# A fused two-block layer on one core: how the in-projection's matmuls are dealt out among the steps of a recurrence

## The reference

```
h  = x * (1 + scale) + shift                 # scale, shift, gate = silu(c) @ mod_w[l] + mod_b[l]
a, r0, k0, v0, wd, ad, gate = split(h @ ev_w_in)
for d in (forward, backward):
    r, k, v = token_shift(r0), token_shift(k0), token_shift(v0)
    decay, a = lora(wd), lora(ad)
    S = S * decay + (S @ a) b^T + v k^T      # one 64 x 64 state for each of 16 heads
    y = S @ r;  y = group_norm(y) + bonus
out = concat(pool(a), y_fwd + y_bwd) * silu(gate) @ ev_w_out
```

## Time and profile before

| what | value |
|---|---|
| median of three runs | 3863.41 us |
| the profiled execution, its own time | 3858.04 us |
| its span, first to last instruction | 3856.2 us |
| granted TensorE clock, mean over the span | 0.965 |
| PE busy (matmuls) | 3547.2 us, 92% |
| PEld busy (weight loads) | 2932.6 us, 76% |
| DVE busy | 2038.4 us, 53% |
| ACT busy | 1541.8 us, 40% |
| POOL busy | 250.7 us, 6% |
| the two-lane recurrence with its fill | about 190 to 1440 us of the span |

### The profile page before, as it was taken

How to read it: one execution, slowest core, us unless ns; L and a number is a source line. 1 busy time by engine, 2 the same in 40 slices (tenths; PEclk the granted TensorE clock), 3 DMA queues, 4 the chain that set the end, 5 groups by cost and what they waited for, 6 DMA issues and landing times. The chain is left out here.

```text
span 3856.2 us, 71009 instructions
## 1 busy us (share of the span) xinstructions
PE 3547.2 (92%) x31292; PEld 2932.6 (76%) x31292; DVE 2038.4 (53%) x3564; ACT 1541.8 (40%) x2599; POOL 250.7 (6%) x295
## 2 busy tenths in 40 slices
PE   6788989999898998989999799989999999999998
PEld 3566666766666676768888789847989799999877
DVE  1454454544455447774665556655444555555444
ACT  2333343333333333454544444425443444444433
POOL 0001111011111112002000000010000000000000
PEclk9899999999999999999999799999999999999999
DMA  9423323242333416443325354414553555555554
GB/s 379 144 70 97 112 86 117 70 128 84 117 101 97 128 44 234 151 138 113 109 91 185 128 164 136 154 61 155 184 181 125 175 175 175 182 180 185 190 182 163
DMA packets 349473, 548.57 MB, mean 142 GB/s; under 512 B 11724, under 2 KB 119916, under 8 KB 346988
## 3 DMA queue, kind: packets, MB, share of 16 engines
q1 hardware_dynamic: 346716, 538.78, 42.9%
q10 hardware_dynamic: 2448, 5.24, 0.4%
HBM read 535.86 MB, written 8.13 MB: 141 GB/s over the span
## 5 line engine op out<-in xcount | busy, mean ns | idle before, releaser
L302 PE MATMUL lane<-r,r 128*128 128x256 f32 (+1 forms) x8520 | 1506.9, 326 | 50.4 <-DVE r L260 40.4
L260 DVE TENSOR_TENSOR r<-ring,r 128x1024 fp32r<-128x1024 f32 x770 | 941.2, 1229 | 944.9 <-ACT r L299 943.6
L302 PEld LDWEIGHTS lane<-r,r 128*128 128x128 f32 x8520 | 1279.5, 193 | 207.7 <-DVE r L260 45.7
L302 PE MATMUL bank<-r,r 128*128 128x512 f32 (+2 forms) x6360 | 1402.2, 359 | 36.3 <-DVE r L260 24.8
L302 PEld LDWEIGHTS bank<-r,r 128*128 128x128 f32 x6360 | 1055.0, 195 | 241.9 <-issue 52.2
L299 ACT ACTIVATE r<-ring 128x1024 fp32r<-128x1024 f32 x770 | 808.8, 1056 | 957.1 <-PE lane L302 570.9
L302 PE MATMUL lane<-arena 64*64 64x64 f32 (+4 forms) x12940 | 622.6, 254 | 68.3 <-DVE arena L260 23.9
L302 PEld LDWEIGHTS lane<-arena 64*64 64x64 f32 (+3 forms) x12940 | 468.7, 140 | 234.2 <-issue 111.1
L299 ACT ACTIVATE arena<-lane 128x256 f32<-128x256 f32 (+3 forms) x578 | 248.8, 451 | 558.5 <-PE lane L302 446.4
L260 DVE TENSOR_TENSOR arena<-arena 128x256 f32<-128x256 f32 (+7 forms) x568 | 255.6, 481 | 35.8 <-ACT arena L299 14.9
L271 DVE COPY arena<-lane 128x256 f32<-128x256 f32 (+3 forms) x366 | 131.8, 362 | 267.2 <-PE lane L302 249.6
(11 more groups left out here) (94 smaller groups left out, 1252.2 us busy)
## 6 DMA issues: line engine op xcount, KB each, us to landing
ring<-in_w_gate_up SPq DMA_DIRECT2D x88, 1024.0 KB, 5.0
ring<-in_mod_w SPq DMA_DIRECT2D x73, 1024.0 KB, 5.2
ring<-in_ev_w_in SPq DMA_DIRECT2D x44, 1024.0 KB, 8.4
ring<-in_w_down SPq DMA_DIRECT2D x44, 1024.0 KB, 5.0
ring<-in_od_w_in SPq DMA_DIRECT2D x40, 1024.0 KB, 5.1
ring<-in_w_in SPq DMA_DIRECT2D x40, 1024.0 KB, 5.1
ring<-in_w_xkv SPq DMA_DIRECT2D x32, 1024.0 KB, 5.3
ring<-in_ev_w_out SPq DMA_DIRECT2D x28, 1024.0 KB, 5.2
```

What stands on the lines that cost most here:

```text
L260: return Nothing() if self.e is None else self.e.tensor_tensor(o, a, b, op)
L302: return Nothing() if self.e is None else self.e.matmul(o, l, r, start=start, stop=stop)
```

## The change

The FILL table is larger, the split of a fill between the sources is no longer a share but follows the blocks, and the loads and splits stand elsewhere in the list. The diff, cut to its core:

```
-FILL = {"shift": 4, "kk_sum": 6, "keys": 4.5, "turn_AV": 2, "P_LR": 1, "KR0": 1, "KR1": 1, "solve": 0.5, "GH": 1,
-        "QY": 1, "state0": 2, "state1": 2, "state2": 2, "state3": 2, "centre": 3, "gn_sum": 6, "read_out": 2}
-MOD_SHARE = 0.125
+FILL = {"shift": 5.5, "kk_sum": 7.5, "keys": 6, "turn_AV": 3, "P_LR": 1.5, "KR0": 1, "KR1": 1.5, "double0": 0.5, "solve": 0.5,
+        "GH": 1, "QY": 1, "state0": 2, "state1": 2, "state2": 2, "state3": 2, "centre": 3, "gn_sum": 6.5, "read_out": 3.5}
...
+    def load_mod():
+        if mod_todo and not mod_pieces:
+            l, g, k0 = mod_todo.pop(0)
+            mod_pieces.append((l, g, k0, piece("mod_w", l, k0, 4, g * 512, 512, ring_mod)))
+
     def modulations():
+        while mod_todo or mod_pieces:
+            load_mod()
+            l, g, k0, pc = mod_pieces.pop(0)
             if k0 == 0:
                 b = bank(mod_turn)
             step("mod", l, g, pc, k0, b)
             if k0 == KT - 4:
                 step("mod_row", l, g, b)
-                yield False
+            yield
+            if k0 == KT - 4:
                 step("mod_col", l, g, bank(mod_turn))
...
-                if sm.kind == "gate_in":
-                    step("load_lora", hp)
...
+        def split_next():
+            if not halves:
+                more()
+            if halves:
+                hp, sm, pc, h = halves.pop(0)
+                split_.append((hp, blocks(pc, 1024 * h, h == 1, [(sm, 8 * h + k) for k in range(8)])))
+                if not halves:
+                    more()
+
         while True:
-            while len(split_) < 3:
...
+            if len(split_) < 2:
+                split_next()
...
-            for end in ev_blocks(u, ev_turn):
-                if end and hp is not None and u.blocks[0][0].kind == "gate_in":
+            for j, end in enumerate(ev_blocks(u, ev_turn)):
+                if end and hp is not None and u.blocks[0][0].args[1:] == (2,):
                     made[0] = hp
-                yield end
+                if j == 2:
+                    split_next()
+                    load_mod()
+                yield j == len(u.blocks) - 1
...
         while share[0] >= 1 and sources:
             share[0] -= 1
-            share[1] += MOD_SHARE
-            i = 0
-            if share[1] >= 1:
-                share[1] -= 1
-                i = len(sources) - 1
-            end = next(sources[i], None)
-            if end is None:
+            i = len(sources) - 1 if due[0] else 0
+            due[0] = False
+            end = next(sources[i], "none")
+            if end == "none":
                 sources.pop(i)
-            if end:
-                return
+            elif end:
+                due[0] = True
...
                 for i, w in enumerate(unit(d, hp, seg)):
+                    if i == 4 and d == 0 and seg == 1 and hp + 1 < HPS:
+                        step("load_lora", hp + 1)
...
+    LAST_UNIT = 23 * (2 * HPS - 1) + LAG
-        if ended and x in TAIL:
+        if ended and x in TAIL and rounds > LAST_UNIT:
```

More of the change, by code:

```diff
@@ L869, in order_of_work @@
     ring_ev, ring_mod = Turn([0, 1]), Turn([2])
+    mod_todo = [(l, g, k0) for l, g in [(0, g) for g in range(8, 12)] + [(1, g) for g in range(12)] for k0 in range(0, KT, 4)]
+    mod_pieces = []
+    def load_mod():
+        if mod_todo and not mod_pieces:
+            l, g, k0 = mod_todo.pop(0)
+            mod_pieces.append((l, g, k0, piece("mod_w", l, k0, 4, g * 512, 512, ring_mod)))
     def modulations():
[L872 to L875, removed]
+        while mod_todo or mod_pieces:
+            load_mod()
+            l, g, k0, pc = mod_pieces.pop(0)
             if k0 == 0:
@@ L878, in modulations @@
             step("mod", l, g, pc, k0, b)
-            if i + 1 < len(todo):
-                l_, g_, k_ = todo[i + 1]
-                nxt = piece("mod_w", l_, k_, 4, g_ * 512, 512, ring_mod)
-            yield False
             if k0 == KT - 4:
                 step("mod_row", l, g, b)
-                yield False
+            yield
+            if k0 == KT - 4:
                 step("mod_col", l, g, bank(mod_turn))
-                yield False
+                yield
     big_sums = [(hp, sm) for hp in range(1, HPS) for sm in bigs_of(hp)]
@@ L892, in products @@
     def products():
-        ready_ = []
+        halves, split_ = [], []
         def more():
@@ L905, in more @@
             for h in range(2):
-                ready_.append((hp, sm, pc, h))
-        split_ = []
-        while True:
-            while len(split_) < 3:
[L911 to L916, removed]
+                halves.append((hp, sm, pc, h))
+        def split_next():
[6 more added lines that the diff above has]
+                    more()
+        while True:
+            if len(split_) < 2:
+                split_next()
             if not split_:
@@ L922, in products @@
             hp, u = split_.pop(0)
-            for end in ev_blocks(u, ev_turn):
-                if end and hp is not None and u.blocks[0][0].kind == "gate_in":
+            for j, end in enumerate(ev_blocks(u, ev_turn)):
+                if end and hp is not None and u.blocks[0][0].args[1:] == (2,):
                     made[0] = hp
-                yield end
+                if j == 2:
+                    split_next()
+                    load_mod()
+                yield j == len(u.blocks) - 1
     sources = [products(), modulations()]
-    share = [0.0, 0.0]
+    share, due = [0.0], [False]
     def fill(n):
```

## The result

The changed kernel takes 3782.32 us (median of four runs, 3778.39 to 3790.41), the kernel before beside it 3863.70. The ratio is 0.9788, with a 95% interval of 0.9775 to 0.9800: 82 us faster. The profiled execution has a span of 3776.6 us, 79.6 less than before, at a mean granted clock of 0.971.

The account below looks back on a forecast made before the run. PE bounds the kernel, with 121 us idle and about 100 us at the lower clock in the recurrence. Terms -45 - 12 - 3 - 15 + 12 + 2 = -61 us from 3858 give 3797, stated as 3800; range 3760 to 3845.

Parts of the forecast that it names:

- Part 1: Whole kernel: matmuls, splits and loads the same, modulations in 80 pieces instead of 96 with the same instructions; 0 us.
- Part 2: Recurrence: the new table leaves no bulk of blocks ahead of a pair; moving a bulk wins nothing by itself.
- Part 3: In-projection loads and splits: earlier loads and a later split end most ACT waits; PE wins 45 us (bounds 20 and 60).
- Part 4: Shift, kk_sum, keys, read_out: 1.5 more blocks each win 12 us (5 to 20); half a block in P_LR, KR1 wins 3.
- Part 5: Recurrence: fewer stalls mean less time at the lower PE clock; 15 us won (bounds 5 and 35).
- Part 6: Sum ends: further blocks in the same call wait for ACT to copy bank 0; 12 us lost over 19 ends (0 to 60).
- The 2 us for mod loads: Mod load after the last modulation, one slot, eight blocks between: 2 us lost (0 and 10).
- Rival A: Sum ends in shift, kk_sum or keys: bank wait decides, 87 us instead of 12, time 3877, slower; chance 0.07.
- Rival B: SP queue: block loads go out no earlier; 3862, no difference (chance 0.07), or 3833 with half the effect (0.14).
- Rival C: Recurrence: nearly all idle time goes, 85 us plus 25 from the clock, losses 5, time 3758; chance 0.12.
- Rival D: PE weight loads are the true limit; spread blocks overlap better with small matmuls, 27 us more, 3773; chance 0.03.
- the rule of the Trainium skill on weight loads: Recurrence: weight loads' busy share measures headroom, up to 398 us open; the prediction held a bulk's 70% busy against it.

Follow-up runs that it names:

- the fastest version: Changed kernel with each in-projection load directly ahead of its split, Sum picked later, and fill stopping at a Sum's end: 3760.33 us, 0.9741 of the kernel before.

## Why the prediction was right

The forecast was 3800 us, range 3760 to 3845; measured 3782, at the low end of the 3780 to 3820 that had most of the chance. The sum was -61 us and it was -82. The terms without the clock add up to -46, and PE's idle time fell by 54.4 us; the clock was put at -15, and busy time fell by 26.6. Behind the 54.4 stands more: the waits at the bank rose by 25.1 where 12 were put, so the other idle time fell by 79.5 where parts 3 and 4 had 60. The mechanisms were right, and that the total came near owes something to luck, since a gain and a loss were both put too low. By its steps:

- Part 1, no change in the work: right, the same 16948 matmul records in the recurrence.
- Part 2, no bulk left: right by the planner's list, in which no twelve pieces follow each other without a step of the recurrence. That a moved bulk wins nothing by itself was tried by no run.
- Part 3, the loads, 45 us and most of the clock's 15: mechanism right, size right only roughly. With the old table they bring 37 us of time, and some 50 with the 15 reckoned for the last unit without fill; ACT's 104.5 us are gone. But in idle time that kernel wins 14.1 us, or 22 without its last unit's 8, and the rest is busy time. Under the new table, from 107.0 to 71.9, it is 35.1, although PE waits 28 us more at the bank there. So what the loads save depends on the table, and the 45 as such is not shown. Two statements in it were wrong. I had the load's place nine pieces ahead do it; either load's move alone does it. And the split's later place was counted in; it is worth nothing. What I hadn't seen is how much hangs on it: under the new table, with the modulations in step with the units of blocks, the old places cost 119 us.
- Part 4, the thicker fill, 12 + 3 us: the term that was mis-sized most. The new table alone brings 33 us, in spite of its last unit without fill, and on top of the early loads 45 less the 15 reckoned for the last unit, 30. I had let 1.05 us more of PE work take 1.05 us off a stall and no more, 12 of 27 us; the waits at sums and transposes fell from 61.8 us to 31.0 with the table alone and to 1.5 with the whole change. That the blocks added at shift also hide what is late at kk_sum is my reading of it; no run had more fill in one step alone.
- Part 5, the clock, 15 us: PE's busy time in the recurrence fell by 26.6, inside the bounds of 5 to 35. The early loads with the old table gave 15.9 of it, about the forecast, and the new table on top of them 10.7: stalls that I had left standing in part 4 went, and with them their stretches at 1.2 GHz. By the mean clock of 0.96 and 0.98, 100 us at the lower level became about 48. One reading was loose: the clock did not fall behind the stall of 7.43 us but within it, to 0.50 from 989, while PE stood until 993.2.
- Part 6, 12 us for the bank: the right wait, and twice the size. It rose from 5.9 to 31.0 us, 1.3 us for each of the 19 ends where 0.65 net was put; taking 17.7 us of it away brought 8.4 back at the lanes and gave 10 to 13 in time. So net of what only moves the 12 may hold, which no run shows for the whole. I had only thought of ACT; more than half is DVE's, at the gate. The 2 us for mod loads were 0.

Rival A needed 3.8 us an end and had 1.3. Rival B, loads no earlier, is what the kernel with both loads in their old places shows, though far worse than priced. Rival C had 85 us for parts 3 and 4 and 25 for the clock, and 79.5 and 26.6 were measured: in its gains it was nearer than the forecast, and only its 5 us of losses were far off. Rival D, and with it the rule of the Trainium skill on weight loads that the prediction set against a row: their busy time in the recurrence went from 864.7 to 854.0 us, 72% of the stretch, and in the fastest version 850.0 of 1169, 73%, with only 53.6 us of idle time left there. It stays near the 70% of the bulk in the earlier trace rows, though the idle time is less than half of the 126.3 us of before, so here matmul idle time and clock were the better measure.

## What to carry to other kernels

A DMA queue that waits on one consumer holds every load behind it: place a load for a slot that is freed late behind those that are wanted soon, and look at what stands between the wait and the next urgent load. When work is handed out in step with another rhythm, count in the list how far apart the two loads and the use come to stand. Work that only fills can be worth more than its own length where it stands ahead of several waits in a row, and where it ends in a buffer that another engine must empty, let a step of other work come before the next piece.

## What the runs showed of the hardware

A stall in which nothing that the profile shows is waited for ("issue") comes in every kernel of the study, up to 3.4 us at a time (in the kernel with the split three units ahead), 16.3 us in 17 pieces in the changed kernel's recurrence and 11.7 in 17 in the fastest, always among the lanes' small matmuls. With the other stalls gone it is now PE's largest wait but one. No run was made for its cause, and it stays open.
